# FFN steps on one core: the low part of each weight slice is multiplied right behind its high part

## The reference

```python
def swiglu(h, w_gate, w_up, w_down):
    return (jax.nn.silu(h @ w_gate) * (h @ w_up)) @ w_down

def conv_ffn(x, g, w_up, dw_w, dw_b, w_down):
    h = causal_depthwise_conv(rms_norm_2(x, g) @ w_up, dw_w, dw_b)
    gate, up = h[..., :D_FF_2], h[..., D_FF_2:]
    return (jax.nn.silu(gate) * up) @ w_down
```

## Time and profile before

| | |
|---|---|
| median of 3 runs | 904.55 us (904.14 to 906.35) |
| span of the profiled execution, first to last instruction | 902.0 us; its own time is not given apart from that |
| granted TensorE clock, mean | 0.998 |
| TensorE matmuls | 5284, busy 886.1 us (98%) |
| weight loads | 5284, busy 783.5 us (87%) |
| VectorE, ScalarE, GpSimd busy | 675.1 us (75%), 482.4 us (53%), 51.6 us (6%) |
| the three FFN layers in the span | about 32 to 203, 322 to 496 and 717 to 893 us |

### The profile page before, as it was taken

The page is one execution under the profiler, slowest core; times in us unless marked ns, Lnnn a source line. Parts: engine busy times, 40 slices in busy tenths (PEclk is TensorE's granted clock), DMA queues, the critical chain, the costliest instruction groups (busy, mean ns, idle before and its releaser), DMA issues.

```text
span 902.0 us, 14533 instructions
## 1 busy us (share of the span) xinstructions
PE 886.1 (98%) x5284; PEld 783.5 (87%) x5284; DVE 675.1 (75%) x1015; ACT 482.4 (53%) x748; POOL 51.6 (6%) x90
## 2 busy tenths in 40 slices
PE   8999999999999999999999999999999999999996
PEld 7888888889998888888888999998898788888885
DVE  5896776777646588767767786986654799999997
ACT  5754444456565665344444635555544665556544
POOL 2300000020000000000000500001100000000000
PEclk9999999999999999999999999999999999999999
DMA  8976766452532758656645775311544566676531
GB/s 252 317 240 196 209 189 178 146 174 83 164 140 94 220 172 257 185 176 202 194 129 189 178 208 169 120 48 70 171 172 124 164 182 187 192 209 187 179 100 48
DMA packets 186599, 153.72 MB, mean 170 GB/s; under 512 B 6113, under 2 KB 171617, under 8 KB 186546
## 3 DMA queue, kind: packets, MB, share of 16 engines
q1 hardware_dynamic: 185794, 150.59, 54.9%
q0 software_dynamic: 752, 2.39, 1.0%
HBM read 151.40 MB, written 1.05 MB: 169 GB/s over the span
## 4 chain that ended last, share of the span: by engine, by line
PE 91%; ACT 4%; DVE 3%; issue 1%; DMA 0%; POOL 0%; POOLq 0%; ACTq 0%; DVEq 0%
PE bank L1954 26%; PE bank L1960 13%; PE bank L1804 13%; PE bank L1806 13%; PE bank L1805 13%; PE bank L1920 2%; PE bank L1821 1%; PE bank L1909 1%; DVE wl L1065 1%; ACT wh L574 1%; PE bank L2302 1%; PE bank L2325 1%; PE bank L2501 1%; PE bank L2480 1%; PE bank L2312 1%
## 5 line engine op out<-in xcount | busy, mean ns | idle before, releaser
L1954 PE MATMUL bank<-xhl,wh 128*128 128x512 f32 x1008 | 252.2, 392 | 0.0
L1954 PEld LDWEIGHTS bank<-xhl,wh 128*128 128x128 f32 x1008 | 184.9, 188 | 37.3
L1960 PEld LDWEIGHTS bank<-xhl,wl 128*128 128x128 f32 x1008 | 137.5, 190 | 9.8
L1960 PE MATMUL bank<-xhl,wl 128*128 128x256 f32 x1008 | 140.5, 282 | 0.0
L660 ACT ACTIVATE wh<-raw 128x2048 fp32r<-128x2048 f32 x57 | 109.0, 1912 | 50.3 <-PE bank L1960 47.4
L1204 DVE TENSOR_TENSOR wl<-raw,wh 128x2048 fp32r<-128x2048 f32 x57 | 130.0, 2281 | 0.2 <-ACT wh L660 0.2
L1065 DVE TENSOR_TENSOR wl<-raw,wh 128x2048 fp32r<-128x2048 f32 (+3 forms) x51 | 104.6, 2061 | 29.1 <-ACT wh L574 29.0
L1806 PE MATMUL bank<-dh,hl 128*128 128x512 f32 x264 | 103.4, 392 | 0.0
L1805 PE MATMUL bank<-dl,hh 128*128 128x512 f32 x264 | 103.1, 390 | 0.0
L1804 PE MATMUL bank<-dh,hh 128*128 128x512 f32 x264 | 102.9, 390 | 0.0
L574 ACT ACTIVATE wh<-raw 128x2048 fp32r<-128x2048 f32 (+3 forms) x52 | 89.9, 1742 | 22.2 <-DMA raw<-in_xattn_wq 5.1
(11 more groups left out here) (323 smaller groups left out, 1551.0 us busy)
## 6 DMA issues: line engine op xcount, KB each, us to landing
raw<-in_ffn_w_up SPq DMA_DIRECT2D x88, 512.0 KB, 6.0
draw<-in_ffn_w_down SPq DMA_DIRECT2D x66, 512.0 KB, 3.5
raw<-in_ffn_w_gate SPq DMA_DIRECT2D x44, 512.0 KB, 5.1
raw<-in_w_in SPq DMA_DIRECT2D x18, 512.0 KB, 5.4
raw<-in_mla_w_o SPq DMA_DIRECT2D x8, 512.0 KB, 3.8
raw<-in_xattn_wv SPq DMA_DIRECT2D x8, 512.0 KB, 4.9
raw<-in_w_out SPq DMA_DIRECT2D x8, 512.0 KB, 3.9
raw<-in_xattn_wq SPq DMA_DIRECT2D x8, 512.0 KB, 5.6
```

Source lines behind the costliest of these rows:

```text
L1954: pe.matmul(b[:, :].rearrange("p (a s) -> p a s", a=2), wh[ns][:, a:a + P], xhl[:, :, k, :], start=k == 0, stop=False, skip_group_check=True)
L1960: ins = pe.matmul(b[:, 0:SEQ], wl[ns][:, a:a + P], xh[:, k, :], start=False, stop=k == KD - 1, skip_group_check=True)
```

## The change

In `up`, the two loops over the eight k tiles become one. Behind each 512-column matmul with the tile of `wh` comes the 256-column matmul with the same tile of `wl`. The wait on `lo_done` moves with the first of them. Sums, banks, start and stop flags of the groups and the semaphore increments stay.

```diff
@@ -1953,10 +1953,8 @@
                             a = (2 * k + half) * P
                             pe.matmul(b[:, :].rearrange("p (a s) -> p a s", a=2), wh[ns][:, a:a + P], xhl[:, :, k, :],
                                       start=k == 0, stop=False, skip_group_check=True)
-                        if half == 0:
-                            pe.wait_ge(lo_done, n + 1)
-                        for k in range(KD):
-                            a = (2 * k + half) * P
+                            if (half, k) == (0, 0):
+                                pe.wait_ge(lo_done, n + 1)
                             ins = pe.matmul(b[:, 0:SEQ], wl[ns][:, a:a + P], xh[:, k, :], start=False,
                                             stop=k == KD - 1, skip_group_check=True)
                         if half == 0:
```

## The result

The changed kernel takes 909.93 us (median of 5 runs, 909.21 to 911.06), the kernel before on the same chip 904.55 (904.14 to 906.35): 1.0058 times as long, with an interval of 1.0047 to 1.0069. It is slower by 0.6%, 5.4 us, where a gain of 2.2 had been forecast, and above the range. The outcome is that of the second rival, though not by the reason that it gave.

What follows compares the result with a forecast made beforehand. TensorE, busy 98% without idle time in the FFN steps, was taken as the bound. Alternation at -0.017 us in 126 halves gave -2.2 us, the moved wait nothing: 904.55 to 902.3 us, range 897.5 to 908.0.

Steps and rivals of the forecast that it cites:

- second rival: In up's halves, 512-column matmuls never reach their settled pace when alternating; slower by over 0.3%, up to 910.5 us; chance 0.20.
- What bounds the kernel: FFN steps: TensorE is 98% busy with no idle before the 512-column matmuls, so a step costs its matmuls one behind another.
- (a): In up, alternating 512- and 256-column matmuls instead of runs of eight: -0.017 us a half in 126 halves, -2.2 us.
- high end: Upper bound for alternating in up: every 512-column matmul as long as the longest, 2.837 us a half, +6.0 us.
- settled sum: A half of up at settled paces, 8 x 0.2267 + 8 x 0.1200 = 2.773 us, against 2.79 measured.
- (b), the wait: In up, the lo_done wait comes 1.6 us earlier in the gate half; priced at nothing, covered by VectorE's two-step lead.
- first rival: In up, weight loads set the 256-column matmuls' pace, so alternating gains 8.2 us: 896.3 us, pair 0.341; chance 0.13.
- unchanged remainder: Outside TensorE's order: VectorE, ScalarE and SyncE's queue keep theirs, clock stays at its upper level, VectorE's products 8.19 us apart.

Runs made afterwards that it cites:

- e3_groups: Changed kernel with 512- and 256-column matmuls in runs of four (layer 0), two (layer 1), mostly three (layer 2) instead of alternating singly; 905.38 us, measured once.
- e12: Changed kernel with the second and third matmul of each gate half exchanged (long, long, short, short at its head); 903.73 us against 905.27 before, ratio 0.9989.
- e7: Changed kernel, halves entered otherwise: two long, two short (layer 0); two long, then short first (layer 1); one long, two short (layer 2); 907.22 us, once.
- e2: Changed kernel, but alternating only layer 0's gate half and layer 1's up half, the rest in runs of eight; 906.52 us against 903.95 before, ratio 1.0029.
- e1: Kernel before the change with only the wait on lo_done moved to before up's second matmul; 904.99 us against 903.95 before, ratio 1.0003.
- e8: Changed kernel with the low product 384 columns wide in layer 0, 128 in layer 1, 512 in layer 2; 960.72 us, measured once.
- e5: Changed kernel with the short matmul first (layer 0), the 512 columns contiguous (layer 1), all matmuls 256 columns wide (layer 2); 909.07 us, measured once.
- e4: Changed kernel with the 256-column matmul using wh's tile (layer 0), streaming xl (layer 1), writing the bank's other half (layer 2); 909.34 us, measured once.

## Why the prediction was wrong

- **What bounds the kernel** was right. In the changed kernel too nothing is waited for in the steps, but for one wait of 0.4 us, and 0.08 us a step goes straight into the time. The earlier trace rows said that there is no idle time to absorb anything.
- **The step that failed** is the last one of (a): "the deviations nearest to our case are those of the first matmul after a switch, +0.008 and -0.006, and in an alternation each matmul is a first one. They nearly cancel". It gave a pair of 0.3467; measured is 0.3533. In the slow pattern the 512-column matmuls last 233 to 241 ns from start to start, 237 on average against 227 settled, which is +0.010; the 256-column ones last 113 to 120, on average 117 against 120, which is -0.003. The surcharge was taken a little too small and the discount twice too large. The sum of the two is not zero but +0.007, five sixths of the way from the forecast to the high end (0.3547). The two sizes had been read from busy times, which the prediction itself calls of no use for a sum; but from start to start they are +0.0066 and -0.0066 (listed in the expectation of `e3_groups`) and give the same 0.3467, so that slip isn't what failed. What failed is taking an alternation for a row of first matmuls. In the quick pattern (e12) it does come out as assumed: the 512-column matmuls take 231 and 233 ns in turn, the 256-column ones 117 and 112, about +0.005 and -0.005 us on average, which cancel. The change as written runs in the other.
- **Behind it stood a wrong model.** The deviations aren't prices of an edge. The same alternation costs 0.3467 or 0.3533 a pair, by what ran ahead of it (e7, e12), halves in the old order become quick behind an alternating one (e2), and `down`, untouched, costs 0.014 more. The prediction's settled sum for a half, 2.773, was right as a floor: it is reached (2.774), only not by the change as written. What it missed is that 0.017 us a half over that floor was there before, in 126 halves, and could be had without interleaving all of them.
- **The second rival** ("the pace never settles") had the mechanism's outward form and its size: its threshold was a pair of 0.3515, its middle 0.352 and 907.8 us, its high end 0.3547 and 910.5 us; measured 0.3533 and 909.9. Its reason, five matmuls to get to the pace, was not it: in the quick pattern an alternation is at 0.3467 at once (e7, from 97.11 on). At 0.20 it had too little weight; the text itself says that what an alternation does at the edges "no row of this trace shows", and then the range should have reached to that rival's bound, 910.5, and not to its nearer half.
- **(b), the wait**, was priced at nothing by a step in the middle of layer 0 and one in layer 2: "the cover is VectorE's lead of two steps" holds there: none of them stalls in any run. It doesn't hold in the first `up` of layer 0, whose slice has no two steps ahead of it; that made its half 0.64 us longer, and by itself, in e1, 0.66. A term small against the range, but one more row, at 33 us, would have shown it.
- **The first rival**, loads setting the pace, needed a pair of 0.341. It is out: the quick pattern stays at 0.3467 (e7, e12). The prediction's condition for a hidden load, that it be shorter than the matmul ahead of it, doesn't fit its own rows: a load is recorded with 0.19 us, and 256-column matmuls run at 0.120 all the same. The length of a load in the records isn't what bounds the pace; how low a load would let it go is known only from 192 columns (0.111) and from the 128 of e8.
- The Trainium skill, "TensorE: Matmul & The Clock Gate", section "Back-to-back issue gap", gives an isolated matmul columns/2.4 + 2.5 ns. An estimate from that is 325 ns for a pair, in any order. The traces don't agree: 347 or 353 by the order, with 349 on average in runs of eight.
- The unchanged remainder was right: other engines, VectorE's 8.19 us a step as the next bound (e5, layer 2), nothing about the clock.

**Still open** is what in TensorE makes the two patterns. Operands, weight tiles, bank halves and the form of the 512 columns are excluded (e4, e5), the wait too (e1). Within `up` it takes unequal widths (e8), but `down`, with 512 columns throughout, takes part as well, and in e8's layer 2 a step of nothing but 512 columns still loses 0.067 us at its heads. Nor was found a rule that tells the pattern from the entry: HHLL gave a quick half in one place and a slow one in another (e7).

## What to carry to other kernels

When an engine has no idle time, an edit that only reorders its instructions is still not free of charge; measure the new order in a piece of the program, since row durations and edge effects of the old order don't add up to it. Where a stream's start-to-start sum lies above its settled paces (here 2.790 against 2.773 us a half), try small exchanges at the head of the group before large reorderings: one exchange of two matmuls was worth 0.6% here. And when a wait is moved forward, look at the first pass through the loop, where the lead of the producer is not yet there or was made by other code.

## What was not expected of the hardware

- Steps bound by TensorE come in whole multiples of 6.67 ns, in every trace here: 8.320 = 1248 of them, 8.400 = 1260, 8.287 = 1243, 8.340 = 1251, 8.373 = 1256, 9.347 = 1402, 10.04 = 1506. Settled matmuls are 34, 26 and 18 of them for 512, 384 and 256 columns, a quick pair 52, a slow pair 53. A step at the settled paces alone would be 1240. Before it has 8 more (2.5 in each half and 3 in `down`), the changed kernel 20 (8 in the gate half, one for each pair, 7 in the up half, 5 in `down`).
- A neighbour's width matters: in the slow pattern 256 beside 512 loses one unit a pair (in the quick one none), 384 beside 512 loses two, and 512 beside 512 none within a half. A whole step of 512 columns still loses ten units, at the head of the gate half, at the end of the up half and in `down`.
- The order in one half changes the time of the next half and of `down`, so a part of a step can't be priced by itself.
- A 512-column matmul can start behind a 128-column one while its own weight load is recorded as running (0.06 us behind the short one's start, the load lasting 0.19), and then takes 0.28 us to the next start. A milder form of this is in the kernel before: in a run of 256-column matmuls each starts 0.12 us behind its load, which lasts 0.19.
